# Inverse roots of the norms: square root on ScalarE and reciprocal on VectorE in place of logarithm and exponential

## The reference, cut to what matters

```python
def rmsnorm(x, w):
    y = x32 * lax.rsqrt(jnp.mean(x32 * x32, axis=-1, keepdims=True) + RMS_EPS)
    return (y * w.astype(jnp.float32)).astype(x.dtype)

def sublayer(x, cond, p, i, mixer_fn):
    h = rmsnorm(x, p['norm_pre'][i]) * (1.0 + scale) + shift
    m, extra = mixer_fn(h)
    return x + gate * rmsnorm(m, p['norm_post'][i]), extra

# in rwkv_mixer, after the scan
    y = ((y - mu) * lax.rsqrt(var + GN_EPS)).reshape(b, s, D_INNER)
    y = y * gn_w + gn_b
    out = ((y + bonus) * jax.nn.silu(g))
```

## Time and profile before

| | |
|---|---|
| median of 3 runs | 4976.1 us (4971.37 to 4978.91) |
| the profiled execution, its own time | 4994.21 us |
| its span, first to last instruction | 4992.4 us |
| granted TensorE clock, mean | 0.956 of full speed |
| TensorE matmuls busy | 4350.3 us, 87% |
| VectorE busy | 2673.4 us, 54% |
| ScalarE busy | 2079.7 us, 42% |
| the two finishes, first centring matmul to VectorE's last instruction | 1561.41 to 1636.09, and to 4860.32 us |

### The profile page before, as it was taken

How to read it: one execution, slowest core, us unless ns; L and a number is a source line. 1 busy time by engine, 2 the same in 40 slices (tenths; PEclk the granted TensorE clock), 3 DMA queues, 4 the chain that set the end, 5 groups by cost and what they waited for, 6 DMA issues and landing times. The chain is left out here.

```text
span 4992.4 us, 135676 instructions
## 1 busy us (share of the span) xinstructions
PE 4350.3 (87%) x60240; PEld 3598.2 (72%) x60240; DVE 2673.4 (54%) x4545; ACT 2079.7 (42%) x3730; POOL 2.7 (0%) x8
## 2 busy tenths in 40 slices
PE   3699997899997879888888799998999889999968
PEld 0398876788885855446666799985888678887848
DVE  0552346777774613135655643357524477777745
ACT  0553214455555533136665500036532245555552
POOL 0000000000000000000000000000000000000000
PEclk7899998999999989989999899999999999999989
DMA  9134584333336110000000011112345843333261
GB/s 417 63 104 126 161 233 144 86 91 92 92 92 162 35 37 29 26 7 1 1 1 26 18 38 42 42 51 72 107 129 158 251 128 86 90 93 91 80 167 64
DMA packets 630869, 465.79 MB, mean 93 GB/s; under 512 B 27553, under 2 KB 606497, under 8 KB 625953
## 3 DMA queue, kind: packets, MB, share of 16 engines
q1 hardware_dynamic: 499488, 391.29, 25.7%
q10 hardware_dynamic: 130816, 66.07, 4.9%
HBM read 333.28 MB, written 123.99 MB: 92 GB/s over the span
## 5 line engine op out<-in xcount | busy, mean ns | idle before, releaser
L663 PE MATMUL ps<-big_r,stage_r 128*128 128x384 f32 x2976 | 642.0, 350 | 16.9 <-DVE big_r L894 15.5
L663 PEld LDWEIGHTS ps<-big_r,stage_r 128*128 128x128 f32 x2976 | 523.1, 189 | 101.9 <-issue 55.7
L2312 PE MATMUL ps<-big_r,w_out 128*128 128x384 f32 x2304 | 417.5, 341 | 48.5 <-DVE w_out L2429 48.2
L2312 PEld LDWEIGHTS ps<-big_r,w_out 128*128 128x128 f32 x2304 | 407.4, 191 | 57.0 <-DVE w_out L2429 51.3
L663 PE MATMUL ps<-big_r,w_slab_r 128*128 128x384 f32 x1488 | 341.4, 337 | 0.0
L415 PE MATMUL ps<-big_r,stage_r 128*128 128x384 f32 x1536 | 309.2, 335 | 18.2 <-DVE big_r L402 18.2
L371 PE MATMUL ps<-arena,w_slab 128*128 128x384 f32 x864 | 294.5, 503 | 27.0 <-DVE arena L1956 24.1
L415 PEld LDWEIGHTS ps<-big_r,stage_r 128*128 128x128 f32 x1536 | 270.5, 188 | 20.5 <-issue 17.9
L371 PEld LDWEIGHTS ps<-arena,w_slab 128*128 128x128 f32 x864 | 169.2, 197 | 152.8 <-issue 46.7
L2108 DVE TENSOR_REDUCE extra<-ps 128x1 f32<-128x1152 f32 (+1 forms) x144 | 171.7, 1234 | 200.3 <-PE ps L2020 200.3
L1437 ACT COPY arena<-ps 128x512 f32<-128x512 f32 x288 | 169.0, 587 | 261.1 <-PE ps L1242 260.7
(11 more groups left out here) (240 smaller groups left out, 8024.1 us busy)
## 6 DMA issues: line engine op xcount, KB each, us to landing
w_slab<-in_w SPq DMA_DIRECT2D x138, 512.0 KB, 3.3
scan_in<-x_resid ACTq DMA_DIRECT2D x112, 576.0 KB, 5.4
arena<-in_w_ada SPq DMA_DIRECT2D x24, 2048.0 KB, 27.4
arena<-scan_in SPq DMA_DIRECT2D x80, 576.0 KB, 7.5
arena<-scan_in SPq DMA_DIRECT2D x144, 320.0 KB, 3.9
arena<-scan_in SPq DMA_DIRECT2D x288, 128.0 KB, 3.9
arena<-scan_in SPq DMA_DIRECT2D x144, 192.0 KB, 4.0
scan_y<-arena SPq DMA_DIRECT2D x144, 128.0 KB, 2.3
```

Source lines behind the costliest of these rows:

```text
L663: mm = pe.matmul(g.ps[:, 3 * s + c, 0:CW], w[:, k * P:(k + 1) * P], x[:, k, chunk(c)], start=k == i == 0, stop=k == NB - 1 and i == 2)
L2312: mm = pe.matmul(g.ps[:, bank(i, b), 0:wide[i]], w[:, b, k * P:(k + 1) * P], r, start=k == j == 0, stop=k == NB - 1 and j == 2)
```

## The change

Each root becomes two steps. ScalarE takes `Sqrt` straight from the PSUM bank, with the division by the count as scale and the epsilon as bias from a second column of `g.eps`. VectorE then takes the reciprocal. VectorE's mean instructions (L334, L2454, L2484) are gone, and so are ScalarE's `Exp` instructions. In the boundary the reciprocal does not stand where the mean stood: it comes right ahead of the first use of the result, in `residual(i, 0)` and `scaled(i, 0)`. The key norm and the attention's norms stay as they were.

```diff
@@ phase_prenorm
-            act.wait_ge(ms_ok, 1)
-            nc.scalar.activation(root, ms, ACT.Ln).then_inc(root_ok, 1)
-            act.wait_ge(root_ok, 1)
-            nc.scalar.activation(rstd, root, ACT.Exp, scale=-0.5).then_inc(rstd_ok, 1)
+            act.wait_ge(sq_used, NB)
+            nc.scalar.activation(as3(root), slot_view(g.ps[:, 0:3, :]), ACT.Sqrt, bias=g.eps[:, 1:2], scale=1.0 / D).then_inc(root_ok, 1)
@@ vector
-            dve.wait_ge(sq_used, NB)
-            nc.vector.tensor_scalar(as3(ms), slot_view(g.ps[:, 0:3, :]), 1.0 / D, RMS_EPS, ALU.mult, ALU.add).then_inc(ms_ok, 1)
+            dve.wait_ge(root_ok, 1)
+            nc.vector.reciprocal(rstd, root).then_inc(rstd_ok, 1)
@@ phase_rwkv_finish, ScalarE
-                    A.activation(root[:, chunk(c)], g.ps[:, var_bank(b, c), 0:CW], ACT.Ln, bias=g.eps[:, 0:1], scale=1.0 / HD).then_inc(ln_ok, 1)
-                act.wait_ge(ln_ok, CH * (b + 1))
-                A.activation(root, root, ACT.Exp, scale=-0.5).then_inc(inv_ok, 1)
+                    A.activation(root[:, chunk(c)], g.ps[:, var_bank(b, c), 0:CW], ACT.Sqrt, bias=g.eps[:, 0:1], scale=1.0 / HD).then_inc(root_ok, 1)
@@ finish(b), VectorE
+                dve.wait_ge(root_ok, CH * (b + 1))
+                V.reciprocal(root, root).then_inc(inv_ok, 1)
                 dve.wait_ge(inv_ok, b + 1)
@@ phase_boundary, ScalarE
             def root1(i):
-                act.wait_ge(ms1_ok, i + 1)
-                A.activation(part(rstd1, i), part(rstd1, i), ACT.Ln).then_inc(ln1_ok, 1)
-                act.wait_ge(ln1_ok, i + 1)
-                A.activation(part(rstd1, i), part(rstd1, i), ACT.Exp, scale=-0.5).then_inc(rstd1_ok, 1)
+                act.wait_ge(sum1_mm, i + 1)
+                if i:
+                    act.wait_ge(x_ok, NB * i)
+                A.activation(part(rstd1, i), g.ps[:, 6, 0:wide[i]], ACT.Sqrt, bias=g.eps[:, 1:2], scale=1.0 / D).then_inc(root1_ok, 1)
@@ residual(i, b), VectorE; scaled(i, b) likewise with rstd2
                 if b == 0:
+                    dve.wait_ge(root1_ok, i + 1)
+                    V.reciprocal(part(rstd1, i), part(rstd1, i)).then_inc(rstd1_ok, 1)
                     dve.wait_ge(rstd1_ok, i + 1)
...
```

More of the change, by code:

```diff
@@ L79, in build @@
         g.extra = sb("extra", [P, T + P])
-        g.eps = sb("eps", [P, 1])
+        g.eps = sb("eps", [P, 2])
         g.flag = sb("flag", [P, 4])
@@ L206, in _ @@
             nc.scalar.activation(sig, cond, ACT.Sigmoid).then_inc(sig_ok, 1)
-            act.wait_ge(set_ok, 4)
+            act.wait_ge(set_ok, 5)
             for i in range(ADA_GROUPS):
@@ L244, in _ @@
         def _(dve):
-            nc.vector.memset(g.eps[:, :], GN_EPS).then_inc(set_ok, 1)
+            nc.vector.memset(g.eps[:, 0:1], GN_EPS).then_inc(set_ok, 1)
+            nc.vector.memset(g.eps[:, 1:2], RMS_EPS).then_inc(set_ok, 1)
             nc.vector.memset(g.flag[:, :], 0.0).then_inc(set_ok, 1)
@@ L248, in _ @@
                 nc.vector.memset(rows[i], 0.0).then_inc(set_ok, 1)
-            dve.wait_ge(set_ok, 4)
+            dve.wait_ge(set_ok, 5)
             dve.wait_ge(sig_ok, 1)
@@ L294, in phase_prenorm @@
     sq = [g.big[2][:, i, :] for i in range(2)]
-    ms, root, rstd = g.big[2][:, 2, :], g.big[2][:, 3, :], g.big[2][:, 4, :]
+    root, rstd = g.big[2][:, 2, :], g.big[2][:, 3, :]
     ada = g.ada[:, layer]
@@ L298, in phase_prenorm @@
         sem = Sems(nc, ctx)
-        sq_ok, sq_used, ms_ok, root_ok, rstd_ok, tmp_ok, h_ok, x_st = sem(
-            "sq_ok", "sq_used", "ms_ok", "root_ok", "rstd_ok", "tmp_ok", "h_ok", "x_stored")
+        sq_ok, sq_used, root_ok, rstd_ok, tmp_ok, h_ok, x_st = sem(
+            "sq_ok", "sq_used", "root_ok", "rstd_ok", "tmp_ok", "h_ok", "x_stored")
         block = ctx.enter_context(nc.Block())
@@ L1722, in phase_rwkv_finish @@
         sem = Sems(nc, ctx)
-        center_ok, yc_mm, sq_ok, var_mm, ln_ok, inv_ok, yn_ok, sum_ok, out_ok = sem(
-            "center_ok", "yc_mm", "sq_ok", "var_mm", "ln_ok", "inv_ok", "yn_ok", "sum_ok", "out_ok")
+        center_ok, yc_mm, sq_ok, var_mm, root_ok, inv_ok, yn_ok, sum_ok, out_ok = sem(
+            "center_ok", "yc_mm", "sq_ok", "var_mm", "root_ok", "inv_ok", "yn_ok", "sum_ok", "out_ok")
         y_in, rest_in = [[sem(f"{n}{i}") for i in range(4)] for n in ("y_in", "rest_in")]
@@ L1758, in variance @@
                     if r >= 2:
-                        pe.wait_ge(ln_ok, r - 1)
+                        pe.wait_ge(root_ok, r - 1)
                     pe.matmul(g.ps[:, var_bank(b, c), 0:CW], g.head_ones[:, :], sq[b % 2][:, chunk(c)], start=True, stop=True).then_inc(var_mm, 1)
@@ L2277, in phase_boundary @@
         wh_ok, wl_ok, row_high_ok, row_ok, unit_mm, m_ok = sem("wh_ok", "wl_ok", "row_high_ok", "row_ok", "unit_mm", "m_ok")
[L2278 to L2281, removed]
+        sq1_ok, acc1_ok, sum1_mm, root1_ok, rstd1_ok, t_ok, x_ok = sem(
+            "sq1_ok", "acc1_ok", "sum1_mm", "root1_ok", "rstd1_ok", "t_ok", "x_ok")
+        sq2_ok, acc2_ok, sum2_mm, last_mm, root2_ok, rstd2_ok, u_ok, h_ok, x_st = sem(
+            "sq2_ok", "acc2_ok", "sum2_mm", "last_mm", "root2_ok", "rstd2_ok", "u_ok", "h_ok", "x_stored")
         slab_in = [sem(f"slab_in{i}") for i in range(WSLOTS)]
@@ L2318, in sum1 @@
                 if i:
-                    pe.wait_ge(ms1_ok, i)
+                    pe.wait_ge(root1_ok, i)
                 pe.matmul(g.ps[:, 6, 0:wide[i]], g.ones[:, :], part(acc1, i), start=True, stop=True).then_inc(sum1_mm, 1)
@@ L2324, in sum2 @@
                 if i:
-                    pe.wait_ge(ms2_ok, i)
+                    pe.wait_ge(root2_ok, i)
                 pe.matmul(g.ps[:, 7, 0:wide[i]], g.ones[:, :], part(acc2, i), start=True, stop=True).then_inc(sum2_mm, 1)
@@ L2336, in _ @@
             if not last:
-                pe.wait_ge(ms2_ok, LAST)
+                pe.wait_ge(root2_ok, LAST)
                 for b in range(NB):
@@ L2380, in root2 @@
             def root2(i):
[L2381 to L2384, removed]
+                if i < LAST:
+                    act.wait_ge(sum2_mm, i + 1)
+                else:
+                    act.wait_ge(last_mm, NB)
+                if i:
+                    act.wait_ge(u_ok, NB * i)
+                A.activation(part(rstd2, i), g.ps[:, 7, 0:wide[i]], ACT.Sqrt, bias=g.eps[:, 1:2], scale=1.0 / D).then_inc(root2_ok, 1)
             def shifted(i, b):
@@ L2450, in add1 @@
                 V.tensor_tensor(part(acc1, i), first, part(sq1[b % 2], i), op=ALU.add).then_inc(acc1_ok, 1)
-            def mean1(i):
-                dve.wait_ge(sum1_mm, i + 1)
-                V.tensor_scalar(part(rstd1, i), g.ps[:, 6, 0:wide[i]], 1.0 / D, RMS_EPS, ALU.mult, ALU.add).then_inc(ms1_ok, 1)
             def residual(i, b):
                 if b == 0:
+                    dve.wait_ge(root1_ok, i + 1)
+                    V.reciprocal(part(rstd1, i), part(rstd1, i)).then_inc(rstd1_ok, 1)
                     dve.wait_ge(rstd1_ok, i + 1)
@@ L2477, in add2 @@
                 V.tensor_tensor(part(acc2, i), first, part(sq2[b % 2], i), op=ALU.add).then_inc(acc2_ok, 1)
[L2479 to L2484, removed]
             def scaled(i, b):
                 if b == 0:
+                    dve.wait_ge(root2_ok, i + 1)
+                    V.reciprocal(part(rstd2, i), part(rstd2, i)).then_inc(rstd2_ok, 1)
                     dve.wait_ge(rstd2_ok, i + 1)
@@ L2500, in _ @@
                         low_slab_of(b + 2)
-                    if i and b == 0:
-                        mean1(i - 1)
                     if i < LAST:
@@ L2512, in _ @@
                             add2(i - 1, NB - 1)
-                        if b == 6 and not last:
-                            mean2(i - 1)
                         if b == 7 and i < LAST and not last:
@@ L2517, in _ @@
                                 scaled(i - 1, k)
-            mean1(LAST)
             if not last:
@@ L2524, in _ @@
             if not last:
-                mean2(LAST)
                 for b in range(NB):
```

## The result

The changed kernel takes **5066.28 us** (median of 4 runs, 5064.87 to 5067.5), the kernel before on the same chip 4975.95 us (4 runs, 4971.37 to 4978.91). The ratio is 1.0175 with an interval of 1.0163 to 1.0187: **slower by 90 us**.

The account below looks back on a forecast made before the run. The prediction took ScalarE to bound the finish before and VectorE after; its terms 105.0 + 5.5 + 5.2 + 15.4 + 1.7 + 0.9 = +133.7 us gave 5110 us against the median of 4976.1, range 5050 to 5169.

Parts of the forecast that it names:

- What bounds the finish: In the finish, ScalarE sets the pace before at 7.32 us a block; VectorE sets it after at 13.94 us.
- The price of the reciprocal: Wide reciprocals on VectorE: 8 ns a column, 9.37 us for 1152 columns and 3.22 us for 384.
- Finishes: Two finishes of eight blocks, VectorE taking 13.94 us a block: 53.2 + 51.8 = +105.0 us.
- prenorm: From last sum to first product in the prenorm, 10.53 us in place of 5.06: +5.5 us.
- chunk 0: Chunk 0's norm 1 inside chunk 1: 1.7 us reach TensorE in each of three boundaries, +5.2 us.
- tails: Boundary tails from VectorE's last addition to the residual: 10.3 us against 5.22, three times, +15.4 us.
- norm 2 of the last chunk: In three boundaries, 3.85 us in place of 3.30: three times 0.55, +1.7 us.
- chunk 1: In the boundaries, VectorE has a lighter list for chunk 1 with no rows to split: nothing added.
- the load before `Tanh`: New table load costs nothing because ScalarE waits there anyway; two loads, 2.6 us, if that cover were gone.
- Rival 1: Reciprocal at ordinary 1.04 ns a column; loads bound the finish, 27 us saved in all, 4949 us; chance 0.11.
- Rival 2: Reciprocal passes two columns at a time, 4 ns a column; finish's block 9.33 us, 5011 us; chance 0.07.
- The even point: Finish even at about 2.5 ns a column, reciprocal 2.8 us + 4.5 = 7.3, today's pace; chance 0.02.

Follow-up runs that it names:

- experiment 5: Gate product of the finish moved from VectorE to GpSimd: in the changed kernel 5040.15 us (1.0146), in the kernel before 4970.56 us (1.0009).
- experiment 3: Changed kernel plus scratch reciprocals of several widths and sources and a GpSimd product in the prenorm; 6.25 ns a column from 8 to 512, 164 and 166 ns at 1 and 2.
- experiment 2: Changed kernel with all 38 wide reciprocals cut to 128 columns into a spare tile, so results are no norms: 4950.04 us, 0.9958.
- experiment 4: Changed kernel with the finish's reciprocal cut to 384 columns, 4969.08 us, or 768 columns, 5017.2 us; one run each.
- the halves: Kernel before with only the finish changed, 5038.53 us (+68.2 us), and with only prenorm and boundaries changed, 4984.65 us (+14.3 us).
- experiment 7: Kernel before with logarithm from the bank, finish's centred copy and squares on VectorE, gate product on GpSimd: 4976.95 us; with TensorE's order also turned, 4973.77 us.
- experiment 7's second kernel: The spread finish over three engines with TensorE's order turned, the next block centred ahead of this block's sums: 4973.77 us, 1.0008.

## Why the prediction was right, and where its size was off

- **What bounds the finish** (ScalarE before, VectorE after, by its list without a gap): right. The timeline has no wait between blocks, and experiment 5 shows it from both sides.
- **The price of the reciprocal: the term that was mis-sized.** "I take 8 ns a column, a little under the upper bound since a part of the 9 ns may be fixed": it is 6.25 ns, 7.35 and 2.55 us in place of 9.37 and 3.22. The 9 ns of a one-column form were read as a slope, and experiment 3 shows a floor there. That the value fell inside 1.04 to 10 ns was the bounds' doing, not the row's. That the measured time lies in the forecast's range has luck in it: the range went down to 6 ns a column, a figure for which no row spoke, and 6.25 lies just above it, as 5066 us lies 16 above the lower end of 5050. The Trainium skill's repeat count of 8 ("VectorE: DVE Perf Modes", section "First, the fixed hardware budget") was on the right side, but the 8.3 ns a column worked out from it are not what these runs show: 6.25 ns is six times 1.04.
- **The sum, with the measured price put in.** Finishes 2 x 8 x (7.35 + 4.57) - 118.05 = +72.7; prenorm +3.45; chunk 0 3 x 1.06 = +3.2; tails 3 x 3.8 = +11.3; norm 2 of the last chunk -0.4; last tail +0.2: **+90.5 us**, and 90.3 were measured. The measured difference is known to some 6 us either way, so the agreement to 0.2 is chance, but no large term is missing: of the sum's 133.7 us the price alone takes 43 away.
- **By phase:** finishes +36.4 and +34.9 us (predicted 53.2 and 51.8; at 6.25 ns 37.0 and 35.7). Prenorm: root to first product 169.30 to 177.94 is 8.64 us against 5.06, +3.6. Boundaries +4.6, +4.5 and +5.1 against 4.7 each; of these the tail gives 3.6. In the three boundaries TensorE's matmuls waited 5.4 us in 6 waits for the late sums of norm 2 where it was 1.7 in 3. Of this chunk 0's norm 1 makes 1.0 a boundary, against 1.06; the prediction's nothing for chunk 1 was off by 0.2 us.
- **Costed at nothing, the load before `Tanh`:** rightly. In the changed kernel it starts at 211.29, and behind it ScalarE still waits 4.99 us for TensorE, where it waited 6.29 before: the load fits into the wait.
- **Rival 1**: its price was wrong by a factor of 5, its mechanism right. With a cheap reciprocal the loads do take over (experiment 2). That the total of 4950 is its 4949 is luck: it had 27 us saved and 7.7 of them in each finish, and 20 were saved, with 4.5 and 5.9 in the finishes. **Rival 2** (4 ns): excluded. The even point near a reciprocal of 2.8 us agrees with experiment 4; that is 2.3 ns a column and not the 2.5 that stands beside it in the prediction.
- **What stays open:** the 8 us between the sum of the halves and the whole, within what the runs can tell, and the rest of experiment 7's miss.

## What to carry to other kernels

A form's price per column can't be read from a row of one column: take it from a wide row, or run two widths before building on it. When work leaves the engine that sets the pace, its new engine's whole list must be summed: here 3.7 us of relief became 7.35 us on an engine with 2.8 us of slack. And a change has parts: reading the bank with scale and bias was worth 5 us by itself, while the square root and reciprocal bundled with it cost some 95.

## What the runs showed of the hardware

- VectorE's reciprocal in f32: 148 ns + 6.25 ns a column from 8 to 1152 columns, 164 and 166 ns at 1 and 2, the same within 12 ns from PSUM and on 64 partitions. That is six times the slope of a product, 1.04 ns a column.
- A VectorE product of two SBUF operands that began during a GpSimd product waited until that was done, 1.26 us a block, in all eleven cases of experiment 7's second kernel. The reciprocal, with one operand, didn't wait and held nothing up, in the timeline of the changed kernel with the gate product on GpSimd:

```profile
1588.54 7.35 DVE L1794 RECIPROCAL arena<-arena 128x1152 f32<-128x1152 f32 x1
1588.70 2.61 POOL L1813 TENSOR_TENSOR arena<-arena 128x1152 f32<-128x1152 f32 x1 [7.79 <-DVE arena L1801]
```

  The Trainium skill, "SBUF — State Buffer", section "Who interferes with whom", states both: the two engines share a pair of ports, which is an exclusive lock; a VectorE instruction with two SBUF inputs contends with a GpSimd instruction that reads SBUF, and one with at most one SBUF input, outside the 2-port modes, does not. Both traces agree with it (1807 against 548 ns; 7.35 and 2.61 us unchanged). Here the reciprocal had begun first; in experiment 3 those of 2 to 256 columns began while GpSimd's product ran, and took 166 to 1753 ns, within 6 ns of the line 148 + 6.25 a column. Experiment 7's expectations had left it out.
- GpSimd's product of 1152 columns takes 2.61 us, 1.9 times VectorE's 1.36.
